# Earlier sum of the last shift weights, and twelve filler products among one-column products, at the start of a two-block transformer kernel

## The reference

```python
def modulation(c, w, b):
    return jnp.split(jax.nn.silu(c) @ w + b, 3, axis=-1)

def sandwich(x, mod, g_pre, g_post, fn):
    shift, scale, gate = mod
    h = rms_norm(x, g_pre) * (1.0 + scale[:, None]) + shift[:, None]
    return x + gate[:, None] * rms_norm(fn(h), g_post)
...
        x = sandwich(x, modulation(c, ada_w[layer, 0], ada_b[layer, 0]), norm_pre[layer, 0], norm_post[layer, 0], mixer)
```

## Time and profile before

| what | value |
|---|---|
| median of 3 runs | 1478.31 us (1476.14 to 1478.85) |
| profiled execution, first to last instruction | 1476.3 us |
| mean granted TensorE clock | 0.984 |
| TensorE matmuls busy | 96% of the span |
| TensorE weight loads busy | 84% |
| VectorE busy | 79% |
| ScalarE busy | 56% |
| HBM traffic | 225 GB/s over the span |

### The profile page before, as it was taken

How to read it: one execution, slowest core, us unless ns; L and a number is a source line. 1 busy time by engine, 2 the same in 40 slices (tenths; PEclk the granted TensorE clock), 3 DMA queues, 4 the chain that set the end, 5 groups by cost and what they waited for, 6 DMA issues and landing times.

```text
span 1476.3 us, 22969 instructions
## 1 busy us (share of the span) xinstructions
PE 1411.3 (96%) x8746; PEld 1243.8 (84%) x8746; DVE 1173.0 (79%) x1800; ACT 829.0 (56%) x1210; POOL 1.2 (0%) x5
## 2 busy tenths in 40 slices
PE   7989999999999999999999889999999999999997
PEld 6988788888998979999979768888879998888886
DVE  5898787897866667598579887799988966879997
ACT  2442544544443446545675436788766564678874
POOL 0000000000000000000000000000000000000000
PEclk8999999999999999999999899999999999999999
DMA  9982489997575515656634134899954544589992
GB/s 367 341 309 92 141 314 346 344 329 243 176 228 158 190 53 164 193 174 185 201 115 144 57 108 167 309 380 381 380 184 115 171 115 157 184 322 383 374 365 83
DMA packets 184480, 333.76 MB, mean 226 GB/s; under 512 B 13340, under 2 KB 127796, under 8 KB 184372
## 3 DMA queue, kind: packets, MB, share of 16 engines
q1 hardware_dynamic: 184372, 332.31, 65.1%
HBM read 331.18 MB, written 1.09 MB: 225 GB/s over the span
## 4 chain that ended last, share of the span: by engine, by line
PE 74%; DVE 13%; DMA 6%; ACT 3%; issue 3%; SPq 1%; DVEq 0%; ACTq 0%
PE PSA L642 14%; PE PSA L645 13%; PE PSA L647 13%; PE PSA L646 13%; PE PSB L645 5%; PE PSB L647 5%; PE PSB L646 5%; PE PSB L642 4%; DVE WL L1996 3%; DMA WR<-ffn_w_in 2%; DVE ACC L1993 2%; DVE T L1996 1%; DVE AR L1996 1%; DMA WR<-hyb_w_in 1%; ACT WH L1475 1%
## 5 line engine op out<-in xcount | busy, mean ns | idle before, releaser
L1996 DVE TENSOR_TENSOR WL<-WR,WH 128x1024 fp32r<-128x1024 f32 x352 | 422.6, 1220 | 101.0 <-ACT WH L1475 100.4
L1475 ACT CAST WH<-WR 128x1024 fp32r<-128x1024 f32 x352 | 357.6, 1050 | 113.7 <-DMA WR<-hyb_w_in 44.0
L645 PE MATMUL PSA<-XHL,WH 128*128 128x256 f32 x976 | 282.8, 290 | 8.7 <-DVE WL L1996 2.5
L646 PE MATMUL PSA<-XHL,WH 128*128 128x256 f32 x976 | 277.1, 284 | 0.0
L647 PE MATMUL PSA<-XHL,WL 128*128 128x256 f32 x976 | 277.0, 284 | 0.0
L645 PEld LDWEIGHTS PSA<-XHL,WH 128*128 128x128 f32 x976 | 188.2, 193 | 14.1 <-issue 5.2
L1996 DVE TENSOR_TENSOR WL<-AR,WH 128x1024 fp32r<-128x1024 f32 x152 | 178.4, 1220 | 14.1 <-ACT WH L1475 14.1
L646 PEld LDWEIGHTS PSA<-XHL,WH 128*128 128x128 f32 x976 | 188.2, 193 | 0.9 <-issue 0.5
L647 PEld LDWEIGHTS PSA<-XHL,WL 128*128 128x128 f32 x976 | 188.1, 193 | 0.0
L645 PE MATMUL PSB<-WH,GH 128*128 128x512 f32 x400 | 160.1, 400 | 3.7 <-DVE GL L1996 3.7
L647 PE MATMUL PSB<-WH,GL 128*128 128x512 f32 x400 | 157.2, 393 | 0.0
(11 more groups left out here) (276 smaller groups left out, 2369.7 us busy)
## 6 DMA issues: line engine op xcount, KB each, us to landing
AR<-moe_w_gate_up SPq DMA_DIRECT2D x96, 512.0 KB, 5.9
WR<-ffn_w_in SPq DMA_DIRECT2D x88, 512.0 KB, 4.7
WR<-moe_w_gate_up SPq DMA_DIRECT2D x64, 512.0 KB, 5.7
AR<-ada_w SPq DMA_DIRECT2D x59, 512.0 KB, 9.2
AR<-moe_w_down SPq DMA_DIRECT2D x56, 512.0 KB, 6.0
WR<-ffn_w_out SPq DMA_DIRECT2D x44, 512.0 KB, 4.1
WR<-att_w_qkv SPq DMA_DIRECT2D x36, 512.0 KB, 5.1
AD<-ada_w SPq DMA_DIRECT2D x34, 512.0 KB, 6.2
```

The source lines that it names most:

```text
L645: e.matmul(o, lh, rh, start=start, stop=False, skip_group_check=True)
L646: e.matmul(o, lh, rl, start=False, stop=False, skip_group_check=True)
L1475: A(e.copy(hi_slot(m), raw_slot(m)), s_hi)
L1996: return e.tensor_tensor(o, i, j, op)
```

## The change

TensorE's one-column products of piece 15 come ahead of `ada_total(0)` instead of behind it. Four groups of filler products into bank 5 are added: two products behind piece 14, two behind piece 15, three behind `ada_total(0)`, and five behind the last sums: twelve products, 24 records. Nothing else is changed on any engine.

```diff
@@ -903,16 +903,19 @@
             for x in ADA_BY_PE:
                 if x == ADA_BY_PE[2]:
                     pre(0)
-                if x == ADA_BY_PE[3]:
-                    ada_total(0)
                 e.wait_ge(s_ada[ADA_PLACE[x]].sem, 16 * ADA_COUNT[x])
                 for f in range(8):
                     mm(bank(shifts.b, f, f + 1), ada_at[ADA_PLACE[x]][:, f * P:(f + 1) * P], csil[:, x - 8:x - 7],
                        x == ADA_BY_PE[0] and f == 0, False, skip=True)
+                if x >= ADA_BY_PE[2]:
+                    busy(2, 5)
+            ada_total(0)
+            busy(3, 5)
             e.wait_ge(s_adastep.sem, ada_count(15))
             for f in range(8):
                 t = mm(bank(shifts.b, f, f + 1), accs[1][:, f * P:(f + 1) * P], onesd[:, 0:1], False, f == 7, skip=True)
             t.then_inc(shifts.fill[0], 1)
+            busy(5, 5)
```

## The result

The changed kernel takes 1484.32 us, the median of 22 runs (1474.9 to 1489.95). The kernel before took 1479.06 us in 22 runs beside them (1474.38 to 1484.58). The ratio is 1.0030, with an interval of 1.0018 to 1.0043: 4.4 us slower, 2.7 to 6.4.

A forecast was written before the change was run, and what follows sets the result against it. TensorE's one-column products up to the shift's sums were taken to bound the start: 3.0 us of fillers against 2.0 given back, 1.1 us later, carried to the end in full. Forecast 1479.5 us, range 1476.3 to 1483.6.

The forecast's parts named there:

- the fillers don't hold it: Rival, chance 0.27: TensorE's clock falls at about 30.9 us as before; shift 4.1 to 5.9 us later, 1482.4 to 1484.2 us.
- the forecast case: Likeliest case, chance 0.43: TensorE's clock stays at 2.4 GHz from 24 us on; 1.1 us slower, 1479.5 us.
- the prediction's own signs: Profile after: last sums start near 34.1 us, VectorE's idle ends near 36.0, SyncE's queue released near 42.2, full clock 31 to 41.
- What bounds the start: From 25.98 to 34.86 us the chain of waits lies on TensorE's 64 one-column records, ending with the shift's sums.
- The price of the fillers: Seven fillers ahead of the last sums add 3.0 us at 2.4 GHz; holding the clock gives back 2.0 us.
- the median run loses more: Rival, chance 0.13: in other runs the clock falls a group earlier, so fillers save 0.8 to 2.6 us; 1475.7 to 1477.5.
- I take it that they hold: Seven fillers in TensorE's one-column stretch keep 2.4 GHz, since another filler group follows before 2 us pass, but not by much.
- two groups near 1479 and 1483 us: Times of the changed kernel's runs should split this way if the number of slow products varies from run to run.
- I had the row that told it: Around 1268 us, four filler records, 1.11 us, stood behind 2.22 us of 20-column products, yet the clock went to 0.50.
- I cost the move at 0: Piece 15 ahead of the scale's sums only reorders two groups of 16 records, with both inputs there; cost 0.
- The five behind the last sums: Five fillers after TensorE's last sums fit before the first weight product at 2.4 GHz; cost 0 to 0.5 us.
- The hole in the DMA share: DMA engines run dry at 41 us as SyncE's queue is released; a later release lengthens this one for one.

The follow-up runs named there:

- The kernel before with the weight piece ahead: Kernel before with weight piece 4 loaded ahead of the SyncE load that waits for all eight splits; 1479.67 us, ratio 0.9990 to the kernel before.
- the kernel with the weight piece ahead: Changed kernel with weight piece 4 loaded ahead of the SyncE load that waits for all eight splits; 1484.12 us, ratio 1.0024 to the kernel before.
- The changed kernel with both edits: Changed kernel with opening fillers split eight and six around piece 12 and weight piece 4 loaded before the wait for splits; 1482.68 us, 1.0022 to the kernel before.
- the thin fillers: Changed kernel with each 256-column filler ahead of the last sums replaced by two one-column identity products; 1487.07 us, ratio 1.0046 to the kernel before.

## Why the prediction was right, and where it was not

The measured ratio, put on the median that was shown, gives 1478.31 x 1.0030 = 1482.7 us. It lies in the range of 1476.3 to 1483.6, but only because the range reached into the rival's case: 4.4 us slower is the rival "the fillers don't hold it" (4.1 to 5.9 us), not the forecast of 1.1, whose own range ended at 1480.8. As far as the forecast case goes, that is luck. A chance of 0.70 stood on no difference that can be told, 0.25 on slower, and it is slower. By the prediction's own signs the forecast case failed: the last sums started at 36.57 us and not at 34.1, the shift came at 38.89 and not near 36.0, the queue was let go at 45.07 and not near 42.2, and the windows from 31 us show 0.50 until 37.5.

**What bounds the start** was right. The shift's sums at the end of TensorE's queue set it; a kernel's total roughly follows its shift, from 33.5 us (ratios under 1) to 40.0 us (1.0046), with the single profile of each as the measure. The kernel before with the weight piece ahead stands out, at 37.01 and 0.9990. Its list on TensorE is that of the kernel before, so the late shift belongs to that one execution, in which the clock fell at 27.7 us.

**The price of the fillers**, 3.0 us at 2.4 GHz against 2.0 given back, was right where the clock holds: the kernel without the last five had the shift at 35.74, against a forecast of 35.9. The price at 1.2 GHz was read from the opening, where the products run at half the pace but the view's granted clock says 1.00. It is borne out where the clock reads 0.50: the ten records of the last five fillers take 0.41 us each with the fillers alone (36.84 to 40.89 us). The 2.0 us given back are those of the one execution profiled. In the profile of the kernel before with the weight piece ahead, the same list on TensorE took 11.58 us from piece 14 to the shift instead of 9.04, so there the clock cost 2.5 us more, 4.5 in all (an estimate). Such an execution is what the rival "the median run loses more" had in mind; its saving did not come in the runs.

**"I take it that they hold" is the step that failed.** In the changed kernel's profile the clock fell at 27.2 us, within piece 15's group, with two more groups and five of the seven fillers to come, at double price up to 37.5 us: +4.0 instead of +1.1 us. The fall itself cost more than that difference. From piece 15's start at 26.22 the remaining work takes 12.7 us; at 2.4 GHz it would take 7.5 (three groups of 1.79 and five fillers of 0.43, an estimate from the prices above). The rest was hidden by a queue that stood 3.8 us earlier at piece 14 (22.02 against 25.82). The fall came 1.0 us behind idle time, and this profile alone can't tell whether the idle time or the one-column products brought it. But the kernel with the weight piece ahead, which has the same queue on TensorE and no idle time there, showed a fall at 32.7 us and the shift at 40.51; the one without the last five showed none before its last sums were done. So in the profiles the same seven fillers hold the clock in one case and not in another. That this is what widens the spread of the changed kernel's times is likely and not shown. They don't fall into two groups near 1479 and 1483 us, as the prediction said they should: of the 22, three lie below 1478, five between 1480.5 and 1482.7, thirteen between 1483 and 1488.4. I had the row that told it and read it too lightly.

**"I cost the move at 0"** was wrong in one execution and right in the mean. I had bounded piece 15's landing only by 27.17 us and took its start at 28.4 as given. When the queue is early, TensorE comes to it before 26.2 and stands still with ready work behind it. The changed kernel with both edits shows this too, 0.40 us. The move alone cost nothing that could be measured.

**The five behind the last sums** at 0 to 0.5 us: the traces agree, at either clock, and the runs don't resolve it.

**The hole in the DMA share** grew as was said, from about 1 to about 4 us (the windows from 42 to 46). That it is the path by which the delay travels is shown only in part: a load put into it gave back some 1.4 us, and the changed kernel's chain runs past it over VectorE's WL and TensorE, with no transfer in it. Which way carries how much stays open. The delay itself was carried: by the chain of waits, the group of 16 records that started at 68.40 us before started at 71.92 after, 3.5 us later.

```profile
68.40 1.68 PE PSA L642 x16
```

```profile
71.92 1.68 PE PSA L642 x16
```

**What the runs of before had to say.** I read their spread of 2.7 us as room for a saving. Over 22 runs it was 10 us, and no saving came of it. The page "TensorE: Matmul & The Clock Gate" of the Trainium skill, section "What's actually happening", states that the same kernel shows a varying number of slow products from run to run; it speaks of a kernel's start. The profiles show the like for the falls that follow: nine kernels with the same opening fillers and the same order up to piece 14 showed the first fall anywhere from 17.4 to 27.2 us.

## What to carry to other kernels

A filler that keeps a clock up is paid in full when it stands in the queue that sets the end; here 3.0 us of it stood against 2.0 us to be given back in the execution profiled. Fillers belong where the engine would wait anyway. Before work is taken ahead of other work on an engine, find the landing time of its input by a row, not by where it used to start, and for an execution in which the engine is early. One profile shows one place of the clock's falls: ask what the change is worth with the fall one group sooner and one group later, and weigh the forecast over these.

## What the runs showed of the hardware

TensorE's clock fell while its matmuls and weight loads were both busy 1.00, when the work was one-column products: at 30.9 us before, at 29.5 us with the thin fillers, where it then stayed at 1.2 GHz for 20 us, the last six of them (from 44.1) on weight products of 256 columns. The same seven fillers between the same groups held it up to 37.9 us in one profile (without the last five) and not in three others (27.2 us in the changed kernel, 32.7 with the weight piece ahead, 28.9 in the changed kernel with both edits). In the old order (the fillers alone) it fell at 35.0 us. And the fall of 10 us in the kernel before costs less than it seems: 3.6 against 1.8 us for a group of 16 records, so 1.8 us for each whole group that lies on the path, and nothing for the products from 37 to 41 us: from the shift to the release of SyncE's queue it is 6.17 us with them at 1.2 GHz and 6.18 at 2.4.
